# Streaming encoder layer: norm weights spread by TensorE, first product begun on three tiles, expert weights in other pieces, last rows stored by index

## The reference

```python
h = rms_norm(x, norm_mix_g)
z = h @ w_in                    # pool branch 512 | q 1024 | k 1024 | v 1024 | gates 2048
pool_y, new_pool = pool_mixer(u_pool, ...)        # windows 2, 4, 8, 16
attn = (rms_norm(diff_attend(q, k, v, ...), subln_g) * (1 - lam_init))
merged = sigmoid(gA) * (pool_y @ w_pool_branch) + sigmoid(gB) * (attn @ w_attn_branch)
x = x + merged @ w_out
t = rms_norm(x, norm_ffn_g)     # routing: best of 4 groups, best 2 of its 4 experts
for e in range(16):             # expert e: 1024 -> 512 (gate and up) -> 1024
    hid = silu(t @ w_gate[e]) * (t @ w_up[e])
    y += combine[:, e:e+1] * (hid @ w_down[e])
x = x + y;  y_out = rms_norm(x, final_norm_g)
```

## Time and profile before

| | |
|---|---|
| median of 3 runs | 889.65 us (889.49 to 890.2) |
| the profiled execution | 890.09 us, its span 888.3 us |
| busy, share of the span | PE 94%, PEld 83%, DVE 68%, ACT 58%, POOL 9% |
| mean granted TensorE clock | 0.98 of full |
| DMA | 163.77 MB, mean 184 GB/s over the span, 320 to 344 GB/s in the second half |

### The profile page before, as it was taken

How to read it: one execution, slowest core, us unless ns; L and a number is a source line. 1 busy time by engine, 2 the same in 40 slices (tenths; PEclk the granted TensorE clock), 3 DMA queues, 4 the chain that set the end, 5 groups by cost and what they waited for, 6 DMA issues and landing times.

```text
span 888.3 us, 15492 instructions
## 1 busy us (share of the span) xinstructions
PE 834.4 (94%) x4963; PEld 737.7 (83%) x4963; DVE 603.9 (68%) x1026; ACT 518.5 (58%) x965; POOL 83.7 (9%) x73
## 2 busy tenths in 40 slices
PE   4999999999999999999999998999999999999891
PEld 3999999899989898989997887878777787778670
DVE  6363233687778778466555137689999898998684
ACT  7243214566656666455623232488888788878584
POOL 0000000000000000000000001122233222321020
PEclk9999999999999999999999999999999999999896
DMA  8622222133123212331236746599999999999974
GB/s 260 153 75 80 75 69 72 57 103 85 45 73 102 84 49 78 120 95 49 96 95 210 230 175 228 175 308 337 323 344 342 344 340 338 339 333 335 339 258 156
DMA packets 154392, 163.77 MB, mean 184 GB/s; under 512 B 20596, under 2 KB 138484, under 8 KB 154346
## 3 DMA queue, kind: packets, MB, share of 16 engines
q1 hardware_dynamic: 148538, 151.12, 52.1%
q0 software_dynamic: 5520, 11.45, 4.7%
q10 hardware_dynamic: 288, 0.59, 0.2%
HBM read 151.61 MB, written 20.12 MB: 193 GB/s over the span
## 4 chain that ended last, share of the span: by engine, by line
PE 48%; DVE 5%; DMA 2%; SPq 2%; issue 2%; ACT 1%; POOLq 0%; POOL 0%; DVEq 0%; ACTq 0%
PE ps L1542 14%; PE ps L1544 13%; PE ps L1543 13%; SPq L493 2%; DMA rawM<-in_w_expert_up 1%; PE ps L1906 1%; PE ps L1828 1%; PE ps L1926 1%; PE ps L1835 1%; DVE ob L1513 1%; DMA xg<-h_rows,idi 0%; PE ps L1820 0%; PE ps L1859 0%; DVE wl L1458 0%; PE ps L1860 0%
## 5 line engine op out<-in xcount | busy, mean ns | idle before, releaser
L1458 DVE TENSOR_TENSOR wl<-rawM,wh 128x1024 fp32r<-128x1024 f32 x189 | 223.6, 1220 | 25.3 <-ACT wh L913 23.5
L913 ACT ACTIVATE wh<-rawM 128x1024 fp32r<-128x1024 f32 x192 | 196.0, 1054 | 10.8 <-PE ps L1544 9.0
L1542 PE MATMUL ps<-hTh,wh 128*128 128x272 f32 x448 | 132.2, 295 | 1.6 <-ACT qkv L773 0.9
L1544 PE MATMUL ps<-hTh,wl 128*128 128x272 f32 x448 | 130.4, 291 | 0.0
L1543 PE MATMUL ps<-hTl,wh 128*128 128x272 f32 x448 | 129.7, 289 | 0.0
L1542 PE MATMUL ps<-wh,xh 128*128 128x512 f32 x256 | 105.3, 412 | 4.3 <-issue 4.3
L1543 PE MATMUL ps<-wl,xh 128*128 128x512 f32 x256 | 102.2, 399 | 0.0
L1544 PE MATMUL ps<-wh,xl 128*128 128x512 f32 x256 | 102.2, 399 | 0.0
L1542 PE MATMUL ps<-wh,hTh 128*128 128x384 f32 x256 | 94.5, 369 | 5.1 <-ACT qkv L773 3.6
L1542 PEld LDWEIGHTS ps<-hTh,wh 128*128 128x128 f32 x448 | 85.3, 190 | 3.3 <-ACT qkv L773 1.3
L1544 PE MATMUL ps<-wh,hTl 128*128 128x384 f32 x256 | 86.5, 338 | 0.0
(11 more groups left out here) (300 smaller groups left out, 1682.0 us busy)
## 6 DMA issues: line engine op xcount, KB each, us to landing
rawM<-in_w_expert_gate SPq DMA_DIRECT2D x128, 256.0 KB, 5.2
rawM<-in_w_expert_up SPq DMA_DIRECT2D x128, 256.0 KB, 7.4
rawM<-in_w_expert_down SPq DMA_DIRECT2D x64, 512.0 KB, 8.2
rawA<-in_w_in SPq DMA_DIRECT2D x64, 192.0 KB, 3.0
rawA<-in_w_in SPq DMA_DIRECT2D x20, 512.0 KB, 5.5
rawA<-in_w_attn_branch SPq DMA_DIRECT2D x8, 512.0 KB, 4.1
rawA<-in_w_out SPq DMA_DIRECT2D x8, 512.0 KB, 4.2
x<-in_x_prompt SPq DMA_DIRECT2D x4, 512.0 KB, 6.8
```

The costliest lines, as they stand in the source:

```text
L913: nc.scalar.activation(wh[:, (c + 1) % S, :], rawM[:, slot, :], ACT.Copy).then_inc(m_hi, 1)
L1458: V.tensor_tensor(wl[:, sl, :], rawM[:, slot, :], wh[:, sl, :].bitcast(F32), ALU.subtract).then_inc(m_lo, 1)
L1542: T.matmul(out, sh, mh_, start=start, stop=False, **kw)
L1544: return T.matmul(out, sl, mh_, start=False, stop=stop, **kw)
```

## The change

1. `norm_mix_g` is loaded as one row of 4 KB. PE multiplies a row of 128 ones by it (two float32 products of 512 columns, full precision), and DVE copies the 128 x 1024 result from PSUM to `gb`.
2. SP issues the first weight chunks between the token tiles. PE turns three tiles, begins the first product, and turns tiles 3 and 4 inside its first half, after k = 2 and k = 3. ACT and DVE are put in the matching order.
3. Gate weights come as whole rows (runs of 2 KB): chunks 0 to 3 are gate alone, all 512 columns, in bank 0. Chunks 4, 5 are the first 256 up columns (bank 1), chunks 6, 7 the last 256 (bank 7). One DMA per chunk. ACT does one silu of 512 columns after chunk 3; DVE's `hid` of half 0 now also needs chunk 5 and stands after `ahead(8)`; PE's `turn_hidden(0)` stands after `up(6)`.
4. On PE items 0 to 13 are one loop.
5. Three more DVE operations in the routing make, for every tile, the index of each row, out of range for rows that item 15 owns or that are not prompt rows. Tiles 2 and 3, the last two of `FINAL`, are stored by POOL with these indices, after item 15's rows. POOL now waits for the first three stores alone. ACT and DVE do one more tile before item 15's result.

```diff
-            act.dma_start(gb[:], a["norm_mix_g"][0].partition_broadcast(P)).then_inc(gb_in, 16)
+            act.dma_start(gb[0:1, :], a["norm_mix_g"][0].rearrange("(o n) -> o n", o=1)).then_inc(gb_in, 16)
...
-            dve.wait_ge(gb_in, 16)
+            dve.wait_ge(gain_mm, 1)
+            link(V.tensor_copy(gb[:].rearrange("p (b n) -> p b n", b=2), ps[:, 6:8, :]))
...
+            for b in range(2):
+                ins = T.matmul(ps[:, 6 + b, :], one_row[0:1, :], gb[0:1, 512 * b:512 * b + 512], start=True, stop=True)
+            ins.then_inc(gain_mm, 1)
...
+            for t in range(3):
+                turn_tokens(t)
...
+                        if h == 0 and k in (2, 3):
+                            turn_tokens(k + 1)
...
-                if c < 8:
-                    half, q = divmod(c, 4)
-                    d = d.rearrange("p (k m n) -> p k m n", k=2, m=2)
-                    for m in range(2):
-                        src = moe_src[m][e, 2 * P * q:2 * P * (q + 1), 256 * half:256 * (half + 1)]
-                        sp.dma_start(d[:, :, m, :], src.rearrange("(k p) n -> p k n", p=P)).then_inc(m_raw[slot], 16)
+                if c < 4:
+                    sp.dma_start(d.rearrange("p (k n) -> p k n", k=2), moe_src[0][e, 2 * P * c:2 * P * (c + 1), :].rearrange(
+                        "(k p) n -> p k n", p=P)).then_inc(m_raw[slot], 16)
+                elif c < 8:
+                    half, q = divmod(c - 4, 2)
+                    sp.dma_start(d.rearrange("p (k n) -> p k n", k=4),
+                                 moe_src[1][e, 4 * P * q:4 * P * (q + 1), 256 * half:256 * (half + 1)].rearrange(
+                                     "(k p) n -> p k n", p=P)).then_inc(m_raw[slot], 16)
...
+                act.wait_ge(m_mm, n0 + 5)
+                act.wait_ge(hid_done, 2 * i + 1)
+                nc.scalar.activation(hsl[:], ps[:, 0, :], ACT.Silu).then_inc(si_done, 1)
                 for half in range(2):
-                    act.wait_ge(m_mm, n0 + 4 * half + 5)
-                    act.wait_ge(hid_done, 2 * i + half + 1)
-                    nc.scalar.activation(hsl[:, 256 * half:256 * half + 256], ps[:, half, 0:256], ACT.Silu).then_inc(si_done, 1)
-                    for c in ((7, 8) if half == 0 else (10,)):
+                    for c in ((7, 8, 9) if half == 0 else (10, 11)):
                         ahead(c)
...
+                    dve.wait_ge(m_mm, n0 + 2 * half + 7)
+                    V.tensor_tensor(hid[:, hs], ps[:, UP_BANKS[half], 0:256], hsl[:, hs], ALU.mult).then_inc(hid_done, 1)
...
+                    rows, width = (2, 512) if c < 4 else (4, 256)
+                    bank = 0 if c < 4 else UP_BANKS[(c - 4) // 2]
+                    for kk in range(rows):
+                        k = rows * (c % 4 if c < 4 else c % 2) + kk
+                        wc = slice(width * kk, width * kk + width)
+                        ins = three(ps[:, bank, 0:width], xh[:, k, :], xl[:, k, :], wh[:, (c + 1) % S, wc],
+                                    wl[:, (c + 1) % S, wc], k == 0, k == KD - 1)
...
-            item(0, 0, first=True)
-            item(0, 1)
-            with pe.Fori(1, EXPERTS // 2 - 1) as ip:
+            with pe.Fori(0, EXPERTS // 2 - 1) as ip:
...
-            pool.wait_ge(f_out, 16 * NT)
+            pool.wait_ge(f_out, 16 * 3)
...
+            for j in (3, 4):
+                t = FINAL[j]
+                pool.wait_ge(f_done, j + 1)
+                pool.indirect_dma_start(o["y_prompt"][0], bass.IndirectOffsetOnAxis(ap=kept[:, ORDER.index(t):ORDER.index(t) + 1], axis=0),
+                                        ob[:, t, :], None, bounds_check=SEQ - 1, oob_is_err=False).then_inc(f_late, 16)
```

More of the change, by code:

```diff
@@ L907, in m_hi_split @@
                 slot = 12 * par + c
[L908 removed]
+                act.wait_ge(m_raw[slot], 16 * (rnd + 1))
                 if first:
@@ L977, in item @@
                                          ACT.Copy).then_inc(hid_hi, 1)
-                    for c in ((9,) if half == 0 else (11, 12)):
-                        ahead(c)
+                ahead(12)
                 if final:
@@ L1013, in _ @@
             act.wait_ge(m_lo, 24 * ip + 19)
-            for j in range(3):
+            for j in range(4):
                 final_root(j)
@@ L1461, in item, with hidden, hidden_lo @@
                     ahead(c)
-                for half in range(2):
+                def hidden(half):
+                    hs = slice(256 * half, 256 * half + 256)
+                    if half == 0:
+                        dve.wait_ge(si_done, i + 1)
+                    dve.wait_ge(m_mm, n0 + 2 * half + 7)
+                    V.tensor_tensor(hid[:, hs], ps[:, UP_BANKS[half], 0:256], hsl[:, hs], ALU.mult).then_inc(hid_done, 1)
+                def hidden_lo(half):
                     hs = slice(256 * half, 256 * half + 256)
                     kk = slice(2 * half, 2 * half + 2)
-                    dve.wait_ge(si_done, 2 * i + half + 1)
-                    V.tensor_tensor(hid[:, hs], ps[:, half, 256:512], hsl[:, hs], ALU.mult).then_inc(hid_done, 1)
-                    for c in ((7, 8) if half == 0 else (10,)):
-                        ahead(c)
                     dve.wait_ge(hid_hi, 2 * i + half + 1)
@@ L1471, in item @@
                                     hh[:, kk, :].bitcast(F32), ALU.subtract).then_inc(hid_lo, 1)
-                    for c in ((9,) if half == 0 else (11, 12)):
-                        ahead(c)
+                ahead(7)
+                ahead(8)
+                hidden(0)
+                ahead(9)
+                hidden_lo(0)
+                hidden(1)
+                ahead(10)
+                ahead(11)
+                hidden_lo(1)
+                ahead(12)
                 if final:
@@ L1515, in _ @@
             dve.wait_ge(gb_in, 48)
-            for j in range(2):
+            for j in range(3):
                 final_rows(j)
@@ L1531, in _ @@
             V.tensor_scalar(yb[:, 0, 512:D], xg[:, 1, 512:D], root15[:], None, ALU.mult).then_inc(y15_done, 1)
-            for j in range(2, NT):
+            for j in range(3, NT):
                 final_rows(j)
@@ L1907, in gathered, with item @@
                 ins.then_inc(xg_mm, 1)
-            def item(ip, par, final=False, first=False):
+            def item(ip, par, final=False):
                 i = 2 * ip + par
@@ L1938, in item @@
                 pe.wait_ge(hid_done, 2 * i + 1)
-                for c in range(6):
-                    if first and c == 0:
-                        pe.wait_ge(xg_lo, 1)
-                    elif c == (2 if first else 0):
-                        pe.wait_ge(xg_lo, i + 2)
+                for c in range(7):
+                    if c == 0:
+                        pe.wait_ge(xg_lo, 2 * i + 1)
+                    elif c == 2:
+                        pe.wait_ge(xg_lo, 2 * i + 2)
                     up(c)
                 turn_hidden(0)
-                up(6)
                 up(7)
```

100 lines of the change are left out of this document (64 added, 36 removed).

## The result

The changed kernel takes 893.14 us (median of 7 runs) against 889.79 for the kernel before on the same chip: a ratio of 1.0047, 95% interval 1.0032 to 1.0062: 3.4 us slower by the medians, 4.2 by the ratio. Its profiled execution lasts 892.7 us with a span of 890.4, 2.1 more than before. One run of each kernel lay over 100 us higher; the ratio leaves such disturbed runs out.

A forecast was written before the change was run, and what follows sets the result against it. PE was taken to pace the kernel. Span 888.3 + 1.6 (start) + 8.7 (items) - 2.3 (end) = 896.3 us, 898.1 with the 1.8 around it, 897.6 on the median; 8 in 10 range 889.5 to 901.5.

The forecast's parts named there:

- The start: Up to the second half of the first product: +1.6 us, bounds -1.2 to +3.3 or so.
- Gain products: At the start, PE's two float32 products of 512 columns for the norm weights: 1.8 us each, 3.6 for both.
- The slow clock: At the start, PE starts earlier from idle, so some 6 more products of 272 columns run at half clock: +0.6 us.
- The wait for `hid`: In every item PE waits 0.51 us in front of `turn_hidden(0)`, where it waits not at all today.
- The item: Each expert item +0.58 us, 15 items counted: +8.7 us, bounds 0 to 13.5.
- all of it PE: In the experts' stretch of the kernel before, the 18.34 us from one item's transposes to the next are all PE.
- The 4.33 us and the 2.5 slow clock stay.: Behind the items' loop, PE's idle 4.33 us stay because the jump over the second loop is still there.
- The end: After item 15's rows, POOL waits for only three stores and starts sooner: -2.3 us, bounds -3.5 to 0.
- A: Rival: the stop and slow clock behind the loop are late weights, which longer runs end: -6.8, 890.8 us; chance 0.12.
- B: Rival: the wait for `hid` does not appear, an item costs +0.07: 890.0 us, or 887.2; chance 0.08.
- C: Rival: `hl` misses its 0.2 us margin, or routing and start take upper ends: 0.3 us more per item, 902; chance 0.07.
- D: Rival: the longer loop's code no longer stays near PE, each of 6 jumps back costs a stop: +41, 938 us; chance 0.03.

The follow-up runs named there:

- before_loop: The kernel before with PE, ACT and DVE running the items and spare items in one loop with a count read at run time: 887.24 us, ratio 0.9976.
- one_loop: The changed kernel with items 0 to 13 and the spare items in one run-time-counted loop on PE, ACT and DVE: 888.13 us, ratio 0.9986.
- hid_early: The changed kernel with DVE's order changed: `hid` of half 0 before the split of chunk 8, `hl` before that of chunk 9: 884.24 us, ratio 0.9947.
- best: The changed kernel with parts 1 and 2 undone, `hid` before the split of chunk 8, one run-time-counted loop on PE, ACT and DVE: 881.19 us, ratio 0.9910.
- best_1k: The kernel best with each gate chunk loaded by two DMAs with runs of 1 KB instead of one with 2 KB: 887.35 us, ratio 0.9974.
- best_two: The kernel best with part 2's order at the start, the norm weights still copied by the DMA: 881.75 us, ratio 0.9913.

## Why the prediction was right, and where it was off

Forecast slower, 897.6 us in a range of 889.5 to 901.5; measured slower, 893.14. The mechanism, a wait for `hid` in every item, was right and shown both ways. Most terms were too large, and about 3.7 us of the distance to the likeliest value are clock and stop, which no term had.

- **The start, +1.6 against +2.17.** Gain products 3.75 us (forecast 3.6), first transpose 11.68 (11.5), first product 19.76 (20.0). That 3.6 came so close is luck. The program has one product of 80 columns at L1877, and it leaves two records (as each of the two gain products does, four in all): 0.28 us is the price of one product, not of two, and 512 columns at that rate are 1.8 us each before any half clock. The forecast took half that price and doubled it for a half clock. The half clock was read from durations alone: the windows from 9.70 to 15.20 before and from 5.00 to 8.80 after give a granted clock of 1.00, though the transposes in the first took 0.22 us each and eight behind them (from 15.70, 1.12 us) 0.14. What slowed them stays open. The turns cost 1.3 and 1.0 us (1.0 each). The slow clock was mis-sized against this pair of traces: 6 more products were counted (+0.6), but all 18 ahead of the first turn took 4.24 us (19.76 to 24.00), twice their 0.123 each, where the kernel before had 6, and the window from 22.60 has clock 0.78 where it was 1.00. Before_loop, with the start of before, has 18 such products too, so part of the +2.17 is the execution's; the means over all traces differ by 1.7, near the forecast.
- **The wait for `hid`, 0.51 against 0.38.** Counted from chunk 4, DVE's `hid` starts at 4.15 (forecast 4.2) and PE uses it 0.48 later (0.56). Moving `hid` by one split in either direction moved it as DVE's order says; ACT's 0.26 us ahead of it is in the forecast's chain too.
- **The item, +0.58 against +0.35.** The wait was 0.13 too large, the narrow products cost 0.05 instead of 0.07, and 0.1 was missing that the kernel before lost at each item's boundary. The first is a term's size; the last is a step that failed, "all of it PE", read from a busy share. Over 14 items the three together are 3.0 of the 5.9 us by which the sum was too high.
- **"The 4.33 us and the 2.5 slow clock stay."** They stayed as 3.29 and about 1.6, and the routing's half clock fell from 6.8 to 3.4 us. This was no term of the sum at all: together -3.7 us. The routing's part is luck: the half clock holds 3.4 or 6.8 us in different executions of the same code at that place (before_loop and the kernel before; one_loop and hid_early). Why is open. Behind the loop the kernel before has one trace alone, so its 4.33 and 6.8 us cannot be parted from the execution either; the eight traces of changed kernels that have the stop show 3.3 to 3.8 us.
- **The end, -2.3 against -1.86.** POOL 0.95 behind the rows as said; its starts are 1.42, 1.69 and 1.28 apart instead of 1.33, and from its last DMA to the end of the span it is 4.4 us (forecast 4.1).
- **Rivals.** A (late weights make the stop) is false for the changed kernel, by one_loop. But before_loop shows that the other half of it, weights on their limit, was true of the kernel before. B needed `hid` 0.5 us sooner, and it came 0.13 sooner. C: `hl` was on time but for one 0.2 us wait. D: no stop at the jumps back; from 600 to 780 us the DMA view lists no instruction packet, where the kernel before had one.

## What to carry over

Count what an engine has queued ahead of a result that the pacing engine waits for: one split moved by one place was worth 1.1 us in each item, and the whole change's loss turned to a gain by moving it back. A busy share of 1.00 on PE is no proof that it never waits; compare starts. Before a difference between two traces is given to an edit, look at the same stretch in a trace of the same code: here one start differed by 1.2 us and one routing by 3.4 us of half clock. When a row of the trace is used as a price, count in the program how many instructions stand behind its records. When one engine is made faster, look at once at the lead of the loads: an edit whose worth nothing in the changed kernel showed (longer runs in fewer DMAs) was worth 6 us behind the others.

## What the runs showed of the hardware

- Two float32 products of one row by 512 columns took PE 3.75 us (four records, two for each product, 0.85 to 0.99 us apart).
- Products of 256 columns step at 0.118 us in some items and at 0.1145 in others, both at a granted clock of 1.00 (hid_early: items of 18.25 us with the one, 18.10 with the other). In the changed kernel the wait for `hid` swallows the difference (its rows show 0.22 or 0.38 us, the items all 18.7). What chooses the step was not tested.
- The jump over a skipped loop stopped PE for 3.3 to 4.3 us in all nine traces that have it (in hid_early the row names a split of DVE for it, 3.75 us), with 0 to 6.8 us of half clock in it and behind it, and in none of the five that have not.
- With runs of 2 KB instead of 1 KB, and one DMA instead of two, for a third of the weights the queues moved 343 instead of 334 GB/s from 600 to 780 us (best against best_1k), both at a DMA share of about 1.
- The same code ran at half clock for 3.4 us in one execution and 6.8 in another: in the routing (kernel before 6.8, before_loop 3.4), and at the start, where 6 or 18 of the first 48 products of 272 columns took twice as long.
- When the weights ran late, the last result rows landed late as well: POOL waited 8.2 to 8.7 us for them in best, best_1k, best_two and before_loop, 5.3 to 5.7 in the ten others.
